# An S5 mixer's gelus as y over one plus an exponential, by GpSimd and ScalarE

## The reference, cut to what matters

```python
    y = (jnp.einsum('bsgp,gcp->bsgc', xr, c_re.astype(f32))
         - jnp.einsum('bsgp,gcp->bsgc', xi, c_im.astype(f32))
         + d_skip.astype(f32).reshape(SSM_GROUPS, SSM_GROUP) * ug).reshape(bsz, s, SSM_WIDTH)
    yg = jax.nn.gelu(y)
    out = yg * jax.nn.sigmoid(yg @ w_glu.astype(f32) + b_glu.astype(f32))
```

## Time and profile before

| | us |
|---|---|
| three runs | 1797.25, 1800.06, 1800.57 |
| median | 1800.06 |
| the profiled execution: its time | 1799.23 |
| the profiled execution: its span | 1797.5 |
| TensorE busy | 1710.7 (95%) |
| VectorE busy | 1187.4 (66%) |
| ScalarE busy | 730.1 (41%) |
| GpSimd busy | 465.7 (26%) |

### The profile page before, as it was taken

One profiled execution on the slowest core, in us unless ns is written; L12 is line 12 of the kernel. 1 busy time (PEld: TensorE's weight loads), 2 busy tenths in 40 slices (PEclk: granted clock), 3 DMA queues, 4 the chain that ended last, 5 costly groups with the idle time before them and its releaser, 6 DMA issues.

```text
span 1797.5 us, 21556 instructions
## 1 busy us (share of the span) xinstructions
PE 1710.7 (95%) x7645; PEld 1307.8 (73%) x7645; DVE 1187.4 (66%) x2193; ACT 730.1 (41%) x1176; POOL 465.7 (26%) x448
## 2 busy tenths in 40 slices
PE   7998898899997999999999999999999899999997
PEld 4456654578885888888876887978757588888885
DVE  5976654344446675577556457988884687877786
ACT  3164455533244331133125437566461443333234
POOL 2832200020020110011000114232330266556552
PEclk9999789999998999999999999999999899999999
DMA  6245110043332454455431122121311332423311
GB/s 152 73 98 139 34 60 1 18 118 98 104 130 91 166 176 140 141 186 176 140 117 48 48 59 65 42 59 48 106 47 47 117 117 72 139 71 103 108 42 53
DMA packets 185537, 168.69 MB, mean 94 GB/s; under 512 B 17639, under 2 KB 168867, under 8 KB 185051
## 3 DMA queue, kind: packets, MB, share of 16 engines
q1 hardware_dynamic: 173083, 128.19, 23.4%
q0 software_dynamic: 11808, 39.29, 7.4%
q10 hardware_dynamic: 560, 0.12, 0.0%
HBM read 155.83 MB, written 6.31 MB: 90 GB/s over the span
## 4 chain that ended last, share of the span: by engine, by line
PE 77%; DVE 10%; ACT 7%; issue 3%; DMA 2%; POOL 1%; SPq 0%; DVEq 0%; ACTq 0%; POOLq 0%
PE bank L1508 28%; PE bank L1925 18%; PE bank L1619 3%; PE bank L1813 3%; DVE arena L2680 2%; PE bank L1668 2%; PE bank L1461 2%; PE bank L1447 2%; PE bank L1301 2%; PE bank L1624 2%; PE bank L1403 1%; PE bank L1805 1%; DMA ring<-in_w_in 1%; PE bank L1727 1%; PE bank L1659 1%
## 5 line engine op out<-in xcount | busy, mean ns | idle before, releaser
L3595 DVE SCALAR_TENSOR_TENSOR arena<-bank,ffn_taps,arena 128x441 f32<-128x441 f32 (+2 forms) x352 | 221.3, 689 | 75.7 <-ACT arena L2638 75.4
L3051 DVE TENSOR_TENSOR w_lo<-ring,w_hi 128x2048 fp32r<-128x2048 f32 x52 | 119.2, 2292 | 117.0 <-ACT w_hi L2212 113.2
L1508 PE MATMUL bank<-h_lo,w_hi 128*128 128x512 f32 x448 | 176.5, 394 | 3.2 <-DVE w_lo L3051 1.8
L2212 ACT CAST w_hi<-ring 128x2048 fp32r<-128x2048 f32 x52 | 99.1, 1907 | 176.4 <-PE bank L1508 176.4
L1508 PE MATMUL bank<-hT_hi,w_hi 128*128 128x512 f32 x384 | 153.5, 400 | 6.6 <-DVE h_lo L3137 5.9
L1157 POOL TENSOR_TENSOR w_lo<-ring,w_hi 128x2048 fp32r<-128x2048 f32 x21 | 99.6, 4742 | 165.1 <-ACT w_hi L2611 165.1
L1508 PE MATMUL bank<-act_hi,w_hi 128*128 128x512 f32 x352 | 137.9, 392 | 0.2
L1508 PE MATMUL bank<-act_lo,w_hi 128*128 128x512 f32 x352 | 131.8, 389 | 0.0
L1925 PE MATMUL bank<-hT_hi,w_hi 128*128 128x512 f32 x336 | 130.8, 389 | 0.3 <-POOL w_lo L1157 0.3
L1925 PE MATMUL bank<-hT_hi,w_lo 128*128 128x512 f32 x336 | 130.7, 389 | 0.0
L1925 PE MATMUL bank<-h_lo,w_hi 128*128 128x512 f32 x336 | 130.7, 389 | 0.0
(11 more groups left out here) (578 smaller groups left out, 4020.4 us busy)
## 6 DMA issues: line engine op xcount, KB each, us to landing
ring<-in_w_up SPq DMA_DIRECT2D x76, 512.0 KB, 4.5
arena<-in_w_mod POOLq DMA_DIRECT2D x48, 512.0 KB, 4.2
ring<-in_w_in SPq DMA_DIRECT2D x72, 256.0 KB, 3.1
ring<-in_w_down SPq DMA_DIRECT2D x32, 512.0 KB, 4.1
ring<-in_w_in SPq DMA_DIRECT2D x30, 512.0 KB, 4.0
arena<-in_w_down SPq DMA_DIRECT2D x22, 512.0 KB, 4.3
ring<-in_w_out SPq DMA_DIRECT2D x8, 512.0 KB, 3.9
ring<-in_w_out SPq DMA_DIRECT2D x16, 256.0 KB, 3.0
```

The costliest lines, as they stand in the source:

```text
L1508: ins = pe.matmul(out, u[:, n % SLOTS, cols], v[:, k, :], start=start and k == w[0][0] and m == 0, stop=stop and k == w[-1][0] and m == 2)
L2212: sc.copy(w_hi[:, n % SLOTS, :], ring[:, n % SLOTS, :]).then_inc(hi_ready, 1)
L3051: ve.tensor_tensor(w_lo[:, n % SLOTS, :], ring[:, n % SLOTS, :], value(w_hi[:, n % SLOTS, :]), ALU.subtract)\
L3595: return ve.scalar_tensor_tensor(o[:, ys, xs], x[:, yt, xt], ffn_taps[:, at:at + 1], o[:, ys, xs], ALU.mult, ALU.add)
```

## The change

The gelu is taken apart. GpSimd, once all four skip sums are done, makes u = max(y (1 + 0.044715 y^2), -54) in `gelu_e`, four instructions per quarter. ScalarE takes e = exp(-r u), in place, at pieces 37, 39, 41 and 43, one quarter each. GpSimd then makes e + 1, raises it to the power -1 (the exponent is a tile `minus` of one word, broadcast) and multiplies by y into `gelu_y`. TensorE's gate product waits for these four products (`y_made`). `gelu_e` takes the place of `y_ssm`, which is written later.

```diff
@@ -1,3 +1,4 @@
+import math
 import concourse.bass as bass
 from concourse import mybir
 from contextlib import ExitStack
@@ -93,6 +94,7 @@
 MASKED = 3e38
 ROWS0 = HD
 EXT = ROWS0 + 3
+GELU_FLOOR, GELU_CUBE, GELU_RATE = -54.0, 0.044715, 2.0 * (2.0 / math.pi) ** 0.5
 ROUNDS = HEADS * TT
 V_TILES, VC_TILE = 2 * TT + 1, 2 * TT
 FIRST = ROUNDS // KVG
@@ -301,6 +303,7 @@
         nsign = sb("nsign", [P, 1])
         g_q = sb("g_q", [P, 1])
         eps = sb("eps", [P, 1])
+        minus = sb("minus", [P, 1])
         vec = sb("vec", [P, VEC_COLS])
         ffn_taps = sb("ffn_taps", [P, TAPS * 2 * F2T])
         hc_lo_c, = parts(hc_lo_c=(2, C))
@@ -384,6 +387,7 @@
         y_us = area(0, UT, STEP, CHUNKS)
         gelu_y = area(0, UT, T)
         y_ssm = area(8 * K, UT, T)
+        gelu_e = area(8 * K, UT, STEP, CHUNKS)
 
         qT = area(AT2, 4, T)
         kvT = area(AT2 + 2 * K, 6, T)
@@ -573,8 +577,8 @@
         scr_out, u_in, toep_zero, toep_in = (sem(n) for n in ("scr_out", "u_in", "toep_zero", "toep_in"))
         z_scanned, xprev_ready = sem("z_scanned"), sem("xprev_ready")
         e_swapped, z_swapped = ([sem(f"{n}{k}") for k in range(2)] for n in ("e_swapped", "z_swapped"))
-        s5_full, y_copied, mgate_split, y_in, y_sum, gelu_done, glu_sig, yssm_ready = (
-            sem(n) for n in ("s5_full", "y_copied", "mgate_split", "y_in", "y_sum", "gelu_done", "glu_sig", "yssm_ready"))
+        s5_full, y_copied, mgate_split, y_in, y_sum, gelu_done, glu_sig, y_made = (
+            sem(n) for n in ("s5_full", "y_copied", "mgate_split", "y_in", "y_sum", "gelu_done", "glu_sig", "y_made"))
         silu_ready, mod_used, mod_taken, mod_ready = (
             sem(n) for n in ("silu_ready", "mod_used", "mod_taken", "mod_ready"))
         mod_in = [sem(f"mod_in{k}") for k in range(2)]
@@ -1048,6 +1052,22 @@
             pool.dma_start(y_us, u_scr.rearrange("(m p) s j -> p m s j", p=P)).then_inc(y_in, 16)
             pool.dma_start(yT, y_scr.rearrange("(m p) s j -> p m s j", p=P)).then_inc(y_in, 16)
 
+            step(pool.memset(minus[:], -1.0))
+            pool.wait_ge(y_sum, UT)
+            for m in range(UT):
+                y, u = (x[:, m].rearrange("p s j -> p (s j)") for x in (yT, gelu_e))
+                step(pool.tensor_tensor(u, y, y, ALU.mult))
+                step(pool.tensor_scalar(u, u, GELU_CUBE, 1.0, ALU.mult, ALU.add))
+                step(pool.tensor_tensor(u, u, y, ALU.mult))
+                pool.tensor_scalar(u, u, GELU_FLOOR, None, ALU.max).then_inc(y_sum, 1)
+            for m in range(UT):
+                pool.wait_ge(gelu_done, m + 1)
+                u = gelu_e[:, m].rearrange("p s j -> p (s j)")
+                step(pool.tensor_scalar(u, u, 1.0, None, ALU.add))
+                step(pool.tensor_tensor(u, u, minus[:].to_broadcast([P, T]), ALU.pow))
+                pool.tensor_tensor(gelu_y[:, m, :].rearrange("p (j s) -> p s j", s=STEP), yT[:, m], gelu_e[:, m], ALU.mult)\
+                    .then_inc(y_made, 1)
+
             pool.wait_ge(merged_ready, 2)
             pool.dma_start(ctx_tok, a["ctx_2"][0].rearrange("(t p) c -> p t c", p=P)).then_inc(ctx_in, 16)
             for k, b in enumerate(LEVELS):
@@ -1467,7 +1487,7 @@
                 n = C0["glu"]
                 if m == 0:
                     arrived(n)
-                    pe.wait_ge(gelu_done, UT)
+                    pe.wait_ge(y_made, UT)
                 for k in range(UT):
                     ins = pe.matmul(glu_banks[m][:], slot(n, UT)[:, k, m * P:(m + 1) * P], gelu_y[:, k, :],
                                     start=k == 0, stop=k == UT - 1)
@@ -2232,18 +2252,16 @@
                     exps(UNIT_AT[s])
                 if s == LN_AT:
                     log_sums(1)
-                if s == GELU_AT:
-                    for m in range(UT):
-                        sc.wait_ge(y_sum, m + 1)
-                        sc.activation(gelu_y[:, m, :].rearrange("p (j s) -> p s j", s=STEP), yT[:, m], ACT.Gelu_apprx_tanh)\
-                          .then_inc(gelu_done, 1)
+                if GELU_AT <= s < GELU_AT + 2 * UT and (s - GELU_AT) % 2 == 0:
+                    m = (s - GELU_AT) // 2
+                    sc.wait_ge(y_sum, UT + m + 1)
+                    sc.activation(gelu_e[:, m], gelu_e[:, m], ACT.Exp, scale=-GELU_RATE).then_inc(gelu_done, 1)
                 if s >= MIX_AT and (s - MIX_AT) % 2 == 0 and (s - MIX_AT) // 2 < DT:
                     c = (s - MIX_AT) // 2
                     sc.copy(mix_hi[:, c, :], hT[:, c, :]).then_inc(mix_hi_ready, 1)
                 if s == HIGH_AT:
                     high(C0["merge"], 0, free=True)
             nsa_high(HEADS // 2 - 1)
-            sc.wait_ge(gelu_done, UT)
             for m in range(UT):
                 sc.wait_ge(s5_full, 4 + m + 1)
                 sc.activation(yT[:, m].rearrange("p s j -> p (s j)"), glu_banks[m][:], ACT.Sigmoid,
@@ -2251,7 +2269,7 @@
             n = C0["merge"]
             high(n + 1, 1)
             for m in range(UT):
-                sc.wait_ge(yssm_ready, m + 1)
+                sc.wait_ge(y_made, UT + m + 1)
                 sc.copy(ssm_hi[:, m, :], y_ssm[:, m, :]).then_inc(mix_hi_ready, 1)
 
             def gates(i, first):
@@ -3057,7 +3075,7 @@
             nsa_low(HEADS // 2 - 1)
             for m in range(UT):
                 ve.wait_ge(glu_sig, m + 1)
-                product(y_ssm[:, m, :], gelu_y[:, m, :], yT[:, m].rearrange("p s j -> p (s j)")).then_inc(yssm_ready, 1)
+                product(y_ssm[:, m, :], gelu_y[:, m, :], yT[:, m].rearrange("p s j -> p (s j)")).then_inc(y_made, 1)
             low(C0["merge"] + 1, 1)
             for m in range(UT):
                 ve.wait_ge(mix_hi_ready, DT + m + 1)
```

## The result

The changed kernel takes 2120.76 us (median of four runs, 2116.35 to 2121.89) against 1798.65 (1797.12 to 1800.57): a ratio of 1.178 [1.177, 1.180], 18% slower. The forecast was 1794, in a range up to 1826. The profiled execution took 2116.35 us, 317.1 more than that of before.

A forecast was written before the change was run, and what follows sets the result against it. The prediction took TensorE, busy for 95% of the span, as what bounds the kernel. Its terms, -6.9 + 0.5 + 0 + 0 + 1.0 = -5.4 us, took the profiled 1799.23 us to about 1794, in a range from 1791 to 1826.

The forecast's parts named there:

- the power's price: One GpSimd power of 128x512: taken as 4 us, between 1.3 (a product) and 9.5 (four slowest 128x128 selects).
- GpSimd's second half: After the exponentials, per quarter an addition, power, product and waits: 2.35 us plus the power; hidden, 0 us.
- The budget: From the first exponential's end to the first gate matmul: 32.2 us, 8.05 per quarter, leaving 5.7 us for one power.
- rival 1: Power too slow, TensorE waits at the first gate matmul: 1812 us at 9.5 per power, 1826 at 13; chance 0.38.
- The rule on GpSimd: GpSimd products take about twice VectorE's time; by operations per cycle, a power of 60 operations takes 8.5 us, making it slower.
- The removed block: Two table loads and four gelus leave ScalarE before piece 40: -6.9 us, 4.1 of TensorE waiting and 2.8 of slow clock.
- Exponentials: Four 128x512 exponentials added to ScalarE at pieces 37, 39, 41 and 43: +0.5 us, bounds 0 and 2.7.
- GpSimd's first half: Polynomial behind the last skip sum: 17 us of GpSimd work, hidden, 0 us; would cost beyond twice that price.
- Moved addresses: The new tile shifts all tiles behind it by 32 bytes: transfers on the chain lose +1.0 us, bounds 0 and 5.
- The prediction's own sign for rival 3: Transfers landing later than 3.9 and 4.5 us for the same 512-KB loads would speak for rival 3.
- rival 3: Transfers lose 5 us by the new addresses, and late exponentials cost 2.7, so no gain: 1800 us; chance 0.05.
- The sum: All terms over the whole kernel: -6.9 + 0.5 + 0 + 0 + 1.0 = -5.4 us, giving 1794 us.

The follow-up runs named there:

- e4: Changed kernel, tiles unmoved, floor -27; quarters inverted by GpSimd power in three pieces, VectorE reciprocal whole, same in four, ScalarE exp(-ln(1 + e)): 1854.06 us, one execution.
- e8: Changed kernel with tiles at their old addresses, gelu by tanh, so no power, floor or tile `minus`: 1791.43 us, ratio 0.9963 to the kernel before.
- e3: Changed kernel with tiles at their old addresses, GpSimd's power replaced by a product and plus one by a minimum (output not the gelu): 1795.74 us, ratio 0.9978.
- e1: Kernel before plus only the unused tile `minus`, so all tiles behind it start 32 bytes later: 1810.57 us, ratio 1.0063.
- e2: Changed kernel whole, with `minus` in the place of a pad so that all other tiles keep their old addresses: 2104.97 us, ratio 1.170.
- e6: Kernel before with other pads: everything from `xT` to `ring` moved by 32 bytes, the arena not: 1807.61 us, ratio 1.0048.
- e9: e8 with `minus` declared where the change declares it, so every tile behind lies 32 bytes on: 1805.91 us, ratio 1.0022.

## Why the prediction was wrong, step by step

- **The step that failed** is the power's price, in GpSimd's second half: "I take 4, under 5.7 and nearer to the lower end, because the 30 products and the median select ... lie there." It measured 81.95 us, twenty times that and 8.6 times the upper bound of 9.5. The reason given does not bear on a power at all: products and selects say what passes over memory cost, and a power is arithmetic per element, 160 ns a column in every size (e4). The bound from the slowest select was no bound either.
- **The budget and the form of rival 1** held. Its formula, 4 x (P + 2.35) - 32.2, gives 305 us with P = 81.95; 308.1 were measured. Of the 3 us between, 2.5 are in the quarters, 84.9 us each and not 84.3 (the plus one took 1.50 and not 0.6, the product 1.28 and not 1.45), and 0.6 in the window, 31.6 us and not 32.2. Its "+2.8" for the slow clock came as 2.7. Its place, TensorE's wait at the first gate matmul with GpSimd as releaser, was right. It had 0.38, split over prices up to 13 us, and the top of the range was set by one of them.
- **The rule on GpSimd** pointed the right way (slower), by an estimate of 8.5 us that was still ten times too low. By the Trainium skill's figure of 3 operations per cycle at 1.2 GHz (GPSIMD Engine Reference, Elementwise — side-by-side cycle accounting), 81.95 us for 512 columns are 576 operations an element, an estimate; no row counts them.
- **The removed block**, -6.9: right. The head lost 6.7 us in the changed kernel, with the clock at 1.00, and e8 gained 6.8 over the stage. The 0.2 between is a slip in the marks: 322.76 is a head's second matmul (the first starts at 322.56), while 303.65 is a first.
- **Exponentials, +0.5:** 0 was right. The stretch takes 12.17 us, against 12.23 for the twin that never had gelus, and the next heads none more.
- **GpSimd's first half, 0:** it took 18.6 us (289.60 to 308.22) and not 17, the floor 1.5 us a pass and not 0.6, the square 1.04 and not 1.3. As work it was hidden, as priced; but it cost +1.8 by holding VectorE up (e3, and e8, where it is gone). This route was no term of the sum: "would start to cost beyond twice that price" looked at GpSimd's own clock alone.
- **Moved addresses, +1.0, up to 5:** e1 shows +11 with the tile alone, e2 15.8 less without it. The 5 us bounded the transfers that lay on the chain of the kernel before, and that was the wrong search: in e1 two others, inside the arena, come onto the chain and release VectorE 3.1 us later, and what costs is not that lateness but the clock of 0.50 behind TensorE's wait, 9.3 us by the first head. A change of clock was no part of the term. The prediction's own sign for rival 3 did come, loads of 512 KB landing at 4.8 and 4.0 us where 4.5 and 3.9 stood, but from the merge to the end, where most of these loads are, nothing was lost (-0.9 us). Rival 3 had the direction, at 5 us at most. The rule of the Trainium skill that it cited (DMA: Bandwidth & Descriptors, How a descriptor splits into AXI transactions) adds one transaction to a descriptor off a 256-byte line, be it 32 or 64 bytes off. The loads into `ring` agree in that, 4.8 and 4.9 us, 7 to 9% more, between the 3% and the 25% of the two ways to count; the nine transfers inside the arena scatter too much to tell, and 9.0 us in e6, where the arena did not move, speaks against a price by address alone. The time did not follow either of them.
- **The sum** of -5.4, which had the power for nothing, would by the medians of these runs read -3.8 (e3) + 11.1 (e1) = +7: an estimate for a case that was not run, but it says that the change would not have gained at its own addresses with a free power either; e9, the nearest run, came out at +6.8 by the medians, though its interval does not exclude zero. Faster had 0.45 on the strength of two terms that were taken near their lower ends with no row behind them.

What stays open: why the transfers inside the arena land at such different times (5.6 to 12.9 us), whether TensorE's wait at about 150 us is what lets the clock fall, and which distance between the operands' tiles gives matmuls of 393 ns; none was tried by itself. None of them touches the main result, which the power carries alone.

## What to carry to other kernels

An operation without a row has no upper bound in the rows of cheaper operations; where it stands in front of everything, its price decides the case, and a formula that needs none (here the tanh form, with no inverse) is worth more than an idle engine. An engine that is idle half the time has no room for long instructions if others take short ones from it: compare the length of the piece with the lead, not the sums of busy time. And a declaration moves every tile behind it: put a new small tile in a pad or at the end, and time that alone.

## What was not expected of the hardware

- GpSimd's power costs 160 ns a column of 128 partitions, 64 times its product (1.28 us for 512) and 24 times VectorE's reciprocal. One-operation passes of 128x512 (plus one, maximum) took 1.47 to 1.51 us, e3's minimum 1.81 on average, but a multiply and add in one instruction 0.61 to 0.62 (0.73 on average in e8's second half).
- A product of 48 columns on VectorE took 1.15 us instead of 0.24 because it met a product on GpSimd, and GpSimd's was not lengthened.
- 32 bytes of displacement cost 11 us of 1800 in one kernel and between 1 and 21 in ten executions of another (e9 against e8's median); the executions that lose most are those with the lower granted clock (0.966 to 0.969 against 0.974 to 0.978).
- Matmuls of 128x512 took 393 ns instead of 389 through a whole stage when two groups of tiles had been moved against each other: 7 us.
